# Post-norms of a decoder trunk: sums of squares spread over the partitions by a matrix of ones instead of a spread of finished factors

## The reference

```python
def _rmsnorm(x, g):
    x32 = x.astype(jnp.float32)
    y = x32 * lax.rsqrt(jnp.mean(x32 * x32, axis=-1, keepdims=True) + EPS)
    return (y * g.astype(jnp.float32)).astype(x.dtype)
...
hp = hp + _rmsnorm(mp, norm_mix_post[layer])
hp = hp + _rmsnorm(_swiglu(_rmsnorm(hp, norm_ffn_pre[layer]), w_ffn_gate_up[layer], w_ffn_down[layer]), norm_ffn_post[layer])
```

## Time and profile before

| what | value |
| --- | --- |
| median of 3 runs | 2763.33 us (2760.42 to 2764.66) |
| the profiled execution's own time | 2760.68 us |
| its span | 2758.4 us |
| TensorE busy | 2606.7 us (94%) |
| VectorE busy | 1269.8 us (46%) |
| ScalarE busy | 1030.3 us (37%) |
| GpSimd busy | 1212.0 us (44%) |

### The profile page before, as it was taken

The page is one execution under the profiler, slowest core; times in us unless marked ns, Lnnn a source line. Parts: engine busy times, 40 slices in busy tenths (PEclk is TensorE's granted clock), DMA queues, the critical chain, the costliest instruction groups (busy, mean ns, idle before and its releaser), DMA issues.

```text
span 2758.4 us, 44186 instructions
## 1 busy us (share of the span) xinstructions
PE 2606.7 (94%) x15569; PEld 2328.9 (84%) x15569; DVE 1269.8 (46%) x1761; ACT 1030.3 (37%) x1516; POOL 1212.0 (44%) x608
## 2 busy tenths in 40 slices
PE   6979858999999999999978899999999999999999
PEld 5769547888887788888867599999999999999999
DVE  4466777786887453303456433211243253220234
ACT  4545743432324434323246434222224435222222
POOL 4444243554554335545545224444444334443442
PEclk9989879999999999999989999999999999999999
DMA  6445011233332322333331211232232221232232
GB/s 162 114 104 143 16 57 57 66 101 90 98 102 69 89 84 69 102 90 98 103 106 36 85 55 54 84 92 73 80 89 74 75 73 46 84 91 70 84 88 76
DMA packets 447743, 229.47 MB, mean 83 GB/s; under 512 B 86460, under 2 KB 439440, under 8 KB 447127
## 3 DMA queue, kind: packets, MB, share of 16 engines
q1 hardware_dynamic: 447647, 228.21, 28.9%
HBM read 212.84 MB, written 15.43 MB: 83 GB/s over the span
## 4 chain that ended last, share of the span: by engine, by line
PE 78%; DVE 6%; issue 2%; ACT 2%; POOL 1%; DVEq 0%; ACTq 0%; POOLq 0%
PE psum L704 65%; PE psum L738 3%; PE psum L807 2%; PE psum L977 1%; DVE probs_t L2357 1%; PE psum L1069 1%; DVE scores L2095 1%; DVE top L2088 1%; DVE row_stats L2348 1%; PE psum L1054 1%; PE psum L1077 1%; PE psum L817 1%; PE psum L833 1%; PE psum L1179 1%; PE psum L1126 0%
## 5 line engine op out<-in xcount | busy, mean ns | idle before, releaser
L1839 POOL TENSOR_TENSOR w_lo<-w_raw,w_hi 128x1024 fp32r<-128x1024 f32 (+1 forms) x334 | 854.3, 2558 | 1248.4 <-ACT w_hi L1320 1248.2
L704 PE MATMUL psum<-act_split,w_hi 128*128 128x288 f32 (+1 forms) x6096 | 1344.1, 329 | 13.1 <-POOL w_lo L1839 6.4
L704 PEld LDWEIGHTS psum<-act_split,w_hi 128*128 128x128 f32 x6096 | 980.5, 189 | 99.7 <-issue 5.8
L1320 ACT ACTIVATE w_hi<-w_raw 128x1024 fp32r<-128x1024 f32 (+1 forms) x334 | 374.9, 1123 | 1278.8 <-PE psum L704 1254.9
L704 PE MATMUL psum<-act_split,w_lo 128*128 128x288 f32 (+1 forms) x3048 | 831.6, 327 | 0.0
L704 PEld LDWEIGHTS psum<-act_split,w_lo 128*128 128x128 f32 x3048 | 519.5, 189 | 40.2
L704 PE MATMUL psum<-hidden_split,w_hi 128*128 128x288 f32 (+1 forms) x2112 | 461.4, 327 | 0.0
L704 PEld LDWEIGHTS psum<-hidden_split,w_hi 128*128 128x128 f32 x2112 | 339.4, 188 | 27.5
L704 PE MATMUL psum<-hidden_split,w_lo 128*128 128x288 f32 (+1 forms) x1056 | 287.6, 327 | 0.0
L2416 DVE TENSOR_TENSOR temps<-psum,root_of_input 128x512 f32<-128x512 f32 (+1 forms) x88 | 63.5, 721 | 357.8 <-PE psum L704 343.5
L2422 DVE TENSOR_TENSOR temps<-psum,temps 128x512 f32<-128x512 f32 (+1 forms) x88 | 63.3, 720 | 357.4 <-PE psum L704 332.5
(11 more groups left out here) (290 smaller groups left out, 2347.4 us busy)
## 6 DMA issues: line engine op xcount, KB each, us to landing
w_raw<-in_w_ffn_gate_up SPq DMA_DIRECT2D x352, 256.0 KB, 3.1
w_raw<-in_w_ffn_down SPq DMA_DIRECT2D x64, 384.0 KB, 3.5
w_raw<-in_w_ffn_down SPq DMA_DIRECT2D x64, 320.0 KB, 3.9
w_raw<-in_w_in_odd SPq DMA_DIRECT2D x64, 256.0 KB, 2.9
w_raw<-in_w_in_even SPq DMA_DIRECT2D x60, 256.0 KB, 3.8
w_raw<-in_w_out_odd SPq DMA_DIRECT2D x32, 256.0 KB, 2.9
x_rows<-in_x_prompt SPq DMA_DIRECT2D x8, 512.0 KB, 6.3
w_raw<-in_w_out_even SPq DMA_DIRECT2D x32, 128.0 KB, 2.9
```

What stands on the lines that cost most here:

```text
L704: mm = pe.matmul(PS[:, 2 * p + b, 0:hi - lo], w[:, p, at], x(k)[:, lo:hi], start=(k == 0 and w is WH and x is x_hi), stop=(k == ph.kt - 1 ...
L1320: act.activation(WH[:, p, 0:n], WR[:, p, 0:n], ACT.Copy).then_inc(S("w_hi"), 1)
L1839: pool.tensor_tensor(WL[:, p, 0:n], WR[:, p, 0:n], WH[:, p, 0:n].bitcast(F32), ALU.subtract).then_inc(S("w_lo"), 1)
```

## The change

The sums of squares of seven post-norms are now made with a 128x128 matrix of ones as the stationary operand and the squares as the moving one (`everywhere`), so that each token's sum stands on all 128 partitions, in the banks in which the spread factors stood before. ScalarE takes the root of this whole area in place, VectorE its reciprocal in place. The spread is gone from `post`, and the later `hold` grows from 2 + 5 (2 + 3 at s = 3) products to 11 (5). The pre-norms keep their narrow sums, `root`, `inverse` and `spread`; their count on `n_b` is renumbered. The last post-norm (g = 1, s = 3) stays as it was.

```diff
+        def b_at(g, s):
+            return 2 + 3 * g + s
...
+            def everywhere(src, g, first):
+
+                for lo, hi in ((0, 512), (512, T[1]))[0:g + 1]:
+                    mm = pe.matmul(PSF[:, 2048 + lo:2048 + hi], ONES, src[:, lo:hi], start=first, stop=not first)
+                return mm
...
                 pe.wait_ge(S(f"free_{ph.free[0]}0"), ph.end[ph.free[0], 0])
-                block_sums(norm_at("post", g, s), g, 2)
+                mp = norm_at("post", g, s)
+                pe.wait_ge(S("ss_p"), 7 * (mp + 1))
+                everywhere(SS, g, True)
                 hold(2)
-                spread(r_at(g, SPOST[s]), g)
-                hold(5 if s < 3 else 3)
+                pe.wait_ge(S("sq_p"), 8 * mp + NB)
+                everywhere(SQ[:, 1, :], g, False).then_inc(S("n_sum"), 1)
+                hold(11 if s < 3 else 5)
...
             def post(g, s):
-                root(r_at(g, SPOST[s]), g)
+                if g and s == 3:
+                    root(r_at(g, SPOST[s]), g)
+                    return
+                act.wait_ge(S("n_sum"), r_at(g, SPOST[s]) + 1)
+                b = PSF[:, 2048:2048 + T[g]]
+                act.activation(b, b, ACT.Sqrt, scale=1.0 / D, bias=EPS).then_inc(S("n_rt"), 1)
...
-                act.wait_ge(S("n_b"), r_at(g, SPRE[s]) + 1)
+                act.wait_ge(S("n_b"), b_at(g, s) + 1)
...
-                inverse(r, g)
+                if g and s == 3:
+                    inverse(r, g)
+                else:
+                    dve.wait_ge(S("n_rt"), r + 1)
+                    dve.reciprocal(spread(g), spread(g)).then_inc(S("n_rc"), 1)
...
-                dve.wait_ge(S("n_b"), r + 1)
+                dve.wait_ge(S("n_rc"), r + 1)
```

## The result

The changed kernel takes 2814.82 us (median of 4 runs, 2802.16 to 2822.28) against 2761.88 us before: a ratio of 1.0177, 95% interval 1.0145 to 1.0209. In a second set of runs on another occasion it took 2818.02 us against 2761.55 us, 1.0218 (1.0166 to 1.0271). It is slower, as forecast, but by about 55 us where 25 were forecast, outside the range of 2776 to 2798.

A forecast was written before the change was run, and what follows sets the result against it. The serial post-norm chain was taken to make TensorE wait: 17.9 us of later first scalings plus 7 us of lost clock, 25 us on 2760.68 us; forecast 2787 us, range 2780 to 2796, with B 2776 to 2798.

The forecast's parts named there:

- What bounds a post-norm: Post-norm to next stage: a serial chain where TensorE's wait counts in full and nothing hides a later first scaling.
- Sums and root: At the post-norms: wide sums gain 0 on the path beside the table load; the root takes 0.58 or 0.64 us.
- The size of the reciprocal: VectorE's wide reciprocal at seven post-norms: 8.4 ns an element, 4.45 us for 512 columns and 4.98 us for 576.
- Delay of the first scaling: At seven post-norms the first scaling comes later by 2.35, 2.16, 3.48, 2.0, 3.35, 2.85 and 1.73 us, 17.9 us in sum.
- The clock: TensorE idles between hold and first product; lost clock costs 1.2 us at six places, 7 us in all, bounds 0 and 2.7 each.
- Rival B: TensorE's clock holds through the gaps, so only the 17.9 us of later scalings remain: 2780 us, chance 0.24.
- Rival A: VectorE's reciprocal streams like any other operation, 0.70 and 0.76 us; about 8.5 us gained: 2754 us, chance 0.08.
- C: Steep end of the reciprocal's cost, 6.8 and 7.6 us each, adds 17 us: 2804 us, chance 0.05.
- D: The delay is taken up later because another engine was late in the next stage: about 2763 us, chance 0.03.

The follow-up runs named there:

- run without reciprocal: Changed kernel with the wide reciprocal of the seven post-norms replaced by a multiplication by 1.0 in place: 2761.85 us, ratio 1.0000 against the kernel before.
- without hold: Kernel before with its last hold of 5 products behind the spread taken out at six places: 2806.08 us, ratio 1.0148.
- with few narrow sums: Kernel before with three of four narrow sums left out in six of eight blocks of the first pair, first half only: 2750.05 us, ratio 0.995.
- bridged kernel: Changed kernel with the hold behind the sums lengthened from 11 products to 16 to 26, reaching up to the first product: 2773.61 us, ratio 1.0038.
- second trace: The changed kernel run once more with no edit, for a second trace: 2818.02 us, ratio 1.0218 against the kernel before.

## Why the prediction was wrong

- **What bounds a post-norm, and the sign:** right. The chain is serial, and the wide reciprocal makes it longer than the spread that it replaces.
- **Sums and root:** right. The root takes 0.58 us at 512 columns and 0.64 us at 576, as the squares' rows had it. The root waits for the sums behind the table load at the second place, 0.44 us, where VectorE was late anyway, and 0.08 us at one place of the second half. One slip did no harm: 2.32 us less a tail of 0.4 is 0.19 us for each of ten records, not 0.21; the traces give 0.216 (7.07 less 4.91 us for ten records more), and no row shows the tail apart.
- **The size of the reciprocal:** too high. I drew 8.4 ns an element from rows of one, four and five elements and took 4.45 and 4.98 us; it is 3.37 and 3.77 us. The point of the argument, that it grows with the width far above the 1.1 ns of other operations, holds. The repeat count of 8 in the Trainium skill, "VectorE: DVE Perf Modes", section "First, the fixed hardware budget", gave 8.3 ns as an estimate; the trace does not agree, it shows 6.3 ns an element.
- **Delay of the first scaling:** 1.34, 1.05, 2.38, 1.79, 2.11, 1.69 and 0.50 us, 10.9 in all, where 17.9 were forecast. Six are 1.0 to 1.2 us below, as the reciprocal is. The seventh, g0 s3, is only 0.2 us below, because the mask behind the reciprocal took 1.56 us where the sum had 0.53; behind the multiplication of the run without reciprocal it took 0.48, so it hangs on the wide reciprocal, and why stays open. The trace of before also flatters two places: at g0 s3 and g1 s2 its spread ran at 1.2 GHz, and in the traces of the two edited kernels before (without hold, and with few narrow sums) the first scaling comes 1.6 us earlier there. That could be the 2.8 us that the bridged kernel leaves open. Counted to the first product it is 9.3 us, because at the first two places before, the hold itself had delayed the product; I had put it at the same distance behind the scaling everywhere.
- **The clock:** the step that failed, as a mis-sized term of the sum. "I take 1.2 us at six places, 7 us in all", with a bound of 2.7 us a place. Bridging the gaps gave 44 us back. Measured in the pairs alone: 3.1, 6.9, 8.0, 1.5, 6.2 and 2.9 us, 28.5 in all (31.6 in the second trace), and the first trace lost 18 more in an attention that the second ran without that loss. The gaps were even shorter than I had them, 2.3 to 6.4 us where 3.3 to 7.5 were forecast. The bound came from the two stretches that the trace of before happened to show, behind which TensorE ran a dense hold. The second of them was longer than its window, too: the clock was at 1.2 GHz for 6.8 us there, and the window caught 5.4. I took that length for the most a gap can cause. In the changed kernel a first pair with its narrow sums stayed at half clock for 17.1 us, fully busy all the while, and other traces had 20.5 to 41.0 us. What sets the length is open: less narrow work went with shorter stretches at two places, and at places where nothing changed the length still went from 3.4 to 27.3 us. The trace of before does have a long stretch at half clock, in the attention of the first half, but TensorE is busy for half of it only, so it didn't show this case:

```profile
344.40:385.20 40.80, 21.72 (x82) 17.19 (x83) 32.18 (x92) 16.40 (x46) 15.87 (x21) 0.50 0.20 65
```

- **Rival B** (the clock holds through the gaps) did not occur. Its sum is that of the bridged kernel, 2773.61 us where 2780 was given, low by the reciprocal's error. **Rival A** needed a fast inverse; its 2754 us came with a sum of its own that the run without reciprocal does not bear out (2761.85), since the clock at the two late places was not in it. C and D did not occur. The Trainium skill's statement in "TensorE: Matmul & The Clock Gate", section "HAM oscillation — how this bites in real kernels", that each burst after a wait starts cold, agrees with the trace in kind: at all six places the clock is at 1.2 GHz from between 1.5 us ahead of and 2.6 us behind the first product. It doesn't give the length found here.
- **The chances** had the right sign, with 0.89 on slower, and the range was too narrow because one term's upper end was set by two rows from a different situation.

## What to carry to other kernels

A gap of TensorE costs what runs behind it at half clock, not its own length: gaps of 2.3 to 2.7 us made between 1.5 and 9 us each, and filling six such gaps with products that nobody reads gave 44 us back. So a stretch at half clock that one trace happens to show is no upper bound for the next. Before replacing narrow work by the same work on all partitions, price the one operation that costs most per element, here the reciprocal. If the inverse of a root is wanted everywhere, one activation on the spread sums does it in 0.58 us for 128x512, behind a table load of 1.28 us.

## What was not expected of the hardware

- With TensorE's records busy 27 of 28 us, the granted clock stayed at 1.2 GHz for 17 us in the changed kernel, and it averaged 0.52 over 43 us in the kernel before without its hold. The work there was products of 512 or 288 columns mixed with sums of one column.
- In the one trace taken, gaps of 0.5 to 1.0 us left the clock at full speed at five places, and one of 1.02 us was followed by 3.4 us at 1.2 GHz; gaps of 2.27 to 2.74 us lowered it at every place in each trace that had them.
- How long it then stays down is not fixed by the gap or by the instructions behind it: 3.4, 3.4, 13.7 and 27.3 us at the same place in four traces.
- VectorE's reciprocal of fp32 in PSUM: 3.37 us at 128x512 and 3.77 us at 128x576.
- The changed kernel scatters more from run to run: 2802 to 2835 us in 8 runs, against 2765 to 2779 in 10 with the gaps bridged.
